# A hybrid decoder step on one core: three stages merged into one program per engine, and the attention's value product with its operands exchanged

## The reference, cut to what matters

```python
h = x @ w_in                                    # 1024 -> 8 x 512
# mixer A: 8 heads of 64; for (window, dilation) in (128,1), (512,4), (2048,16):
s = q @ k.T * ATTN_SCALE + rel_bias             # keys at distances 0, d, 2d, ..., window
p = exp(s - max(s)); out = (p / den) @ v        # the three merged by their denominators
# mixer B: 4 heads, state 128x128, gated linear recurrence
S = diag(f_t) @ S + outer(1 - f_t, i_t);  o_t = S.T @ q_t
y = LayerNorm(ALPHA * x + concat(attn * silu(ga), rms(o_b) * silu(gb)) @ w_out)
```

## Time and profile before

| | |
|---|---|
| time, median of 3 runs | 1592.22 us (1588.28 to 1593.67) |
| the profiled execution's own time | 1593.84 us |
| its span, from the first to the last instruction | 1592.0 us |
| mean granted TensorE clock | 0.969 |
| PE busy | 1531.7 us (96%) |
| DVE busy | 767.2 us (48%) |
| ACT busy | 503.4 us (32%) |
| POOL busy | 440.9 us (28%) |
| stage 2's last product | 854.08 us |
| stage 3's first and last product | 857.27 and 1065.87 us |
| stage 4's first product | 1068.51 us |

### The profile page before, as it was taken

One profiled execution on the slowest core, in us unless ns is written; L12 is line 12 of the kernel. 1 busy time (PEld: TensorE's weight loads), 2 busy tenths in 40 slices (PEclk: granted clock), 3 DMA queues, 4 the chain that ended last, 5 costly groups with the idle time before them and its releaser, 6 DMA issues. The chain is left out here.

```text
span 1592.0 us, 25593 instructions
## 1 busy us (share of the span) xinstructions
PE 1531.7 (96%) x9830; PEld 1374.3 (86%) x9830; DVE 767.2 (48%) x1941; ACT 503.4 (32%) x1426; POOL 440.9 (28%) x281
## 2 busy tenths in 40 slices
PE   7999999998999999899998999989899999899998
PEld 7999999996788777677787999979899999788886
DVE  6022110004323224121214699847677777698885
ACT  5111111113200114122322032337677777423321
POOL 1233210000330000000001000018987779344443
PEclk9999999998999999999999599989999999999999
DMA  9999996233786957866665547859696971866642
GB/s 308 338 329 350 343 318 187 81 117 124 210 291 191 313 200 261 299 213 207 202 205 140 114 157 220 257 185 236 138 207 150 202 183 63 286 207 214 219 158 78
DMA packets 174501, 338.34 MB, mean 213 GB/s; under 512 B 15635, under 2 KB 115283, under 8 KB 165523
## 3 DMA queue, kind: packets, MB, share of 16 engines
q1 hardware_dynamic: 141452, 169.18, 35.0%
q10 hardware_dynamic: 22432, 111.29, 22.0%
q0 software_dynamic: 10512, 56.48, 13.3%
HBM read 262.25 MB, written 155.39 MB: 262 GB/s over the span
## 5 line engine op out<-in xcount | busy, mean ns | idle before, releaser
L1394 POOL CAST a_sorted<-a_plain 128x2048 fp32r<-128x2048 f32 x45 | 171.6, 3872 | 240.5 <-POOLq L932 204.8
L251 PE MATMUL acc<-xhi,whi 128*128 128x424 f32 (+1 forms) x640 | 227.3, 355 | 8.6 <-DVE xlo L230 8.6
L759 PE MATMUL nacc<-nwhi,nxhi 128*128 128x512 f32 (+1 forms) x544 | 219.5, 403 | 13.5 <-DVE nwlo L494 7.3
L251 PE MATMUL acc<-xlo,whi 128*128 128x424 f32 (+1 forms) x640 | 226.9, 355 | 0.0
L251 PE MATMUL acc<-xhi,wlo 128*128 128x424 f32 (+1 forms) x640 | 226.8, 354 | 0.0
L759 PE MATMUL nacc<-nwlo,nxhi 128*128 128x512 f32 (+1 forms) x544 | 214.5, 394 | 0.0
L759 PE MATMUL nacc<-nwhi,nxlo 128*128 128x512 f32 (+1 forms) x544 | 214.5, 394 | 0.0
L1659 ACT ACTIVATE a_prob<-a_prob,a_stage 128x256 f32<-128x256 f32 (+1 forms) x384 | 174.1, 454 | 84.2 <-DVE a_stage L1501 81.9
L1501 DVE CUSTOM_DVE_ANT_0 a_prob<-a_banks,a_bias 128x256 f32<-128x256 f32 (+1 forms) x384 | 125.4, 364 | 82.0 <-PE a_banks L1759 73.5
L1784 PE MATMUL a_banks<-a_v,a_probT 128*128 128x64 f32 x1200 | 157.7, 269 | 4.4 <-DVE a_probT L1513 4.4
L1784 PEld LDWEIGHTS a_banks<-a_v,a_probT 128*128 128x128 f32 x1200 | 150.1, 193 | 5.8 <-DVE a_probT L1513 5.0
(11 more groups left out here) (215 smaller groups left out, 2547.3 us busy)
## 6 DMA issues: line engine op xcount, KB each, us to landing
a_plain<-split_qk POOLq DMA_DIRECT2D x48, 512.0 KB, 12.5
out_kwin_s<-in_cache_kT ACTq DMA_DIRECT2D x8, 2048.0 KB, 19.3
split_qk<-spare POOLq DMA_DIRECT2D x16, 1024.0 KB, 14.6
spare<-in_xT SPq DMA_DIRECT2D x32, 512.0 KB, 7.1
projN<-nstage SPq DMA_DIRECT2D x32, 512.0 KB, 6.6
qg<-in_cache_kT ACTq DMA_DIRECT2D x8, 2048.0 KB, 10.6
kf<-in_cache_v ACTq DMA_DIRECT2D x8, 2048.0 KB
out_kwin_s<-in_cache_kT ACTq DMA_DIRECT2D x8, 2032.0 KB, 28.6
```

The costliest lines, as they stand in the source:

```text
L251: mm = pe.matmul(acc[:, j, 0:n], w[:, u, k], x[:, k, c0:c0 + n], start=(k == 0 and a == 0), stop=(k == KD - 1 and a == 2))
L759: mm = pe.matmul(acc[0:m, n % 2], x[:, u, k, 0:m], w[:, k, g * H:(g + 1) * H], start=(k == 0 and b == 0), stop=(k == KD - 1 and b == 2))
L1394: nc.gpsimd.tensor_copy(dst[:, n].rearrange("p (r m) -> p r m", r=d), src[:, n].bitcast(F32).rearrange("p (m r) -> p r m", r=d)).then_inc( ...
```

## The change

It has two main parts and some that go with them.

- Stages 2, 3 and 4 no longer have a `Block` each. Each function returns its five streams as a `Stage`, and `build` opens one `Block` in which every engine runs the streams of the three stages one behind the other. The tiles in PSUM become one shared tile of eight banks, and waits that the meeting points had made needless are written out.
- In `values` the value tile (128 keys x 64) is stationary and the transposed probabilities (128 keys x 128 queries) move. The first block of a unit writes to partitions 0 to 63 and the second to 64 to 127, which are two column halves of the array, and products of the two halves alternate. Four units fill one bank with results that have the queries on the columns. ACT copies it to `oT` (`keep_turned`), PE transposes it in four pieces (`turn_back`) to the same bank, and then `evacuate` copies it to `stage` as before, one step later than before.
- `warm_up` is gone. The scores of the first three attention units are issued by the recurrence's tail, between its last `read_out`s. There the four `turn_keys` of the last segment have a bank each and are issued in a row, and the `delta`s run two ahead. The squares of the last segment's output (`late_squares`) are done by ACT in attention steps 2 to 5.
- SP issues `load_weights(7)` right behind `load_weights(6)`. POOL begins to sort for head 0 while the last segment of the recurrence runs.
- The last `turn_back` stands inside `project(0)`, and ACT's last `evacuate` behind `recurrent_part(1)`.

```diff
-        with nc.Block() as block:
-            @block.tensor
-            def _(pe):
+        def tensor(pe):
...
+        return Stage(sync, gpsimd, vector, scalar, tensor)
...
+        with nc.Block() as block:
...
+            @block.tensor
+            def _(pe):
+                natural.tensor(pe)
+                recurrence.tensor(pe)
+                attention.tensor(pe)
...
                 def turn_keys(s, c):
                     pe.wait_ge(upd_done, NU * (s + 1))
-                    if i >= 1:
+                if s < NSEG - 1 and i >= 1:
                         pe.wait_ge(khn_done, i)
+                if s == NSEG - 1:
+                    pe.wait_ge(khn_done, NCK * s) if c == 0 else pe.wait_ge(mask_done, NA * NSEG - 3 + c)
                     for h in range(HB):
-                        mm = pe.transpose(t_ps[:, h * P:(h + 1) * P], kd[u][:, h, c * CH:(c + 1) * CH], ident[:])
+                    mm = pe.transpose(turned(s, c)[:, h * P:(h + 1) * P], kd[u][:, h, c * CH:(c + 1) * CH], ident[:])
...
                     turn_keys(NSEG - 1, c)
-                for c in range(NCK):
+            for c in range(2):
                     delta(NSEG - 1, c)
+            for c in range(NCK):
                     read_out(NSEG - 1, c)
+                if c + 2 < NCK:
+                    delta(NSEG - 1, c + 2)
+                if c < NCK - 1:
+                    keep["first_scores"](pe, c)
...
                 load_weights(6)
+            load_weights(7)
                 store_partials(NG - 1, 2)
...
                 load_partials(1)
-                load_weights(7)
                 load_gates(2)
...
+            def keep_turned(m):
+                act.wait_ge(pv_done, 4 * (m + 1))
+                if m >= 1:
+                    act.wait_ge(back_done, m)
+                nc.scalar.activation(oT[:].rearrange("p j d -> p (j d)"), o_ps[:, m % 2], ACT.Copy).then_inc(ot_done, 1)
+
                 def evacuate(n):
                     h, c, b = units[n]
-                    act.wait_ge(pv_done, n + 4)
+                act.wait_ge(back_done, n // 4 + 1)
...
-                    if n >= 8 and n % 4 == 0:
-                        evacuate(n - 8)
+                if 2 <= n < 2 + NCK:
+                    first["late_squares"](n - 2)
+                if n == NU + 3:
+                    round_mix(0)
+                if n >= 7 and n % 4 == 3:
+                    keep_turned(n // 4 - 1)
+                if n >= 9 and n % 4 == 1:
+                    evacuate(n - 9)
...
-                    for a, (w, vt, _) in enumerate(ts):
-                        col = (2 * (n % 4) + w) * DA
-                        mm = pe.matmul(o_ps[:, (n // 4) % 2, col:col + DA], probT[:, n % 3, a],
-                                       v[g % 2][:, c, vt, x * DA:(x + 1) * DA],
-                                       start=(a == 0 or ts[a - 1][0] != w), stop=(a == len(ts) - 1 or ts[a + 1][0] != w))
+                first_of = [next(a for a, t in enumerate(ts) if t[0] == w) for w in range(2)]
+                for a, (w, vt, _) in sorted(enumerate(ts), key=lambda t: (t[0] - first_of[t[1][0]], t[1][0])):
+                    mm = pe.matmul(o_ps[w * DA:(w + 1) * DA, (n // 4) % 2, n % 4 * P:(n % 4 + 1) * P],
+                                   v[g % 2][:, c, vt, x * DA:(x + 1) * DA], probT[:, n % 3, a],
+                                   start=(a == first_of[w]), stop=(a == len(ts) - 1 or ts[a + 1][0] != w))
                     mm.then_inc(pv_done, 1)
+            def turn_back(m):
+                pe.wait_ge(ot_done, m + 1)
+                for j in range(4):
+                    mm = pe.transpose(o_ps[:, m % 2, j * P:(j + 1) * P], oT[:, j], ident[:])
+                mm.then_inc(back_done, 1)
...
                 pe.wait_ge(const, 16)
-                warm_up()
-                for n in range(NU + 4):
-                    if n < NU:
-                        scores(n)
+            for n in range(2, NU + 4):
+                if 3 <= n < NU:
+                    scores(pe, n)
...
+                if n >= 9 and n % 4 == 1:
+                    turn_back(n // 4 - 2)
```

More of the change, by code:

```diff
@@ L6 @@
+from collections import namedtuple
 from contextlib import ExitStack
@@ L1173, in attend_and_project @@
+        return Stage(sync, gpsimd, vector, scalar, tensor)
+def attend_and_project(nc, split_qk, projN, rep_p, w_o, attn_s, o_b, norm_g, partials, x_all, ln_g, ln_b, y, copied, first, keep):
     NBK = T // P
@@ L1219, in attend_and_project @@
         probT = sb("a_probT", [P, 3, 4, P])
+        oT = keep["oT"]
         bias.append(sb("a_bias1", [P, 2, NC, 2 * P]))
@@ new lines, in scores @@
+        def scores(pe, n):
+            h, c, b = units[n]
+            g, x = divmod(h, 2)
+            if c == 0 and b == 0:
+                pe.wait_ge(pair_landed[x], 96 * (g + 1))
+            if c > 0 and b == 0:
+                pe.wait_ge(sort_done, 6 * h + 3 * c)
+            source = plain[x] if c == 0 else sorted_[c - 1] if h < HALVES - 1 else (plain[0], sorted_[0])[c - 1]
+            if n < 3:
+                pe.wait_ge(keep["mask_done"], 18 * NSEG)
+                pe.wait_ge(keep["khn_done"], NCK * NSEG)
+            else:
+                pe.wait_ge(p_done, n - 2)
+            for w in range(2):
+                q0, k0, m = block_keys(c, b + w)
+                for a in range(2):
+                    mm = pe.matmul(s_ps[:, n % 3, w * 2 * P + (2 - m) * P:(w + 1) * 2 * P],
+                                   source[:, 0, q0:q0 + P], source[:, 1 + a, k0:k0 + m * P],
+                                   start=(a == 0), stop=(a == 1))
+            mm.then_inc(s_done, 1)
@@ L1849, in _ @@
-                for _ in range(FILL):
-                    pe.matmul(z_ps[1][:, 0, 0:P], ident[:], ident[:], start=True, stop=True)
-                for p in range(1, LAST):
-                    project(p)
-                project_last()
+                            mm = pe.matmul(z_ps[w][:, g], m[:, w, k], ww[:, g * H:(g + 1) * H],
+                                           start=(k == 0 and a == 0), stop=(k == KD - 1 and a == 2))
+                    mm.then_inc(last_half if g == 0 else z_done, 1)
@@ new lines, in tensor @@
+            pe.wait_ge(const, 16)
+            for n in range(2, NU + 4):
+                if 3 <= n < NU:
+                    scores(pe, n)
+                if n == NU + 1:
+                    transposes(0)
+                if 2 <= n < NU + 2:
+                    turn(n - 2)
+                if n >= 4:
+                    values(n - 4)
+                if n >= 9 and n % 4 == 1:
+                    turn_back(n // 4 - 2)
+            project(0)
+            transposes(1)
+            pe.wait_ge(o_out, NU // 4)
@@ L1856, in build @@
+            for _ in range(FILL):
+                pe.matmul(z_ps[1][:, 0, 0:P], ident[:], ident[:], start=True, stop=True)
+            for p in range(1, LAST):
+                project(p)
+            project_last()
+        return Stage(sync, gpsimd, vector, scalar, tensor)
 def build(nc, a, o):
@@ L1876, in build @@
             keep[n] = [sem(f"k_{n}{u}") for u in range(m)]
+        for n in ("q1_done", "a_done", "mask_done", "khn_done", "hs_done", "ho_done"):
+            keep[n] = sem(f"h_{n}")
+        for n in ("group_done", "w_split", "x_split"):
+            first[n] = sem(f"n_{n}")
+        first["sem"] = sem
         right = region(whole, nc)[0]
@@ L1879, in build @@
             keep[n] = right(f"k_{n}", [P, T // P, HB], side="right")
+        first["bounds"], first["ident"] = right("bounds", [P, 4, HB], side="right"), right("ident3", [P, P], side="right")
+        NLM = len(PLEVELS)
+        masks = right("masks", [P, NLM + 2, CH // 2], I32, side="right")
+        first["lmask"], first["dmask"] = masks[:, 0:NLM], masks[:, NLM:NLM + 2].rearrange("p a t -> p (a t)")
+        keep["oT"] = masks[:, 0:8].rearrange("p a t -> p (a t)").bitcast(F32).rearrange("p (j d) -> p j d", j=4)
         with ExitStack() as ctx:
```

2437 lines of the change are left out of this document (1217 added, 1220 removed).

## The result

The changed kernel takes 1607.42 us (median of 4 runs, 1605.88 to 1609.64), the kernel before, with its runs beside it, 1590.25 us. The ratio is 1.0104 with a 95% interval from 1.0090 to 1.0119: slower by 17.2 us. The forecast was 1601 us in a range from 1568 to 1622, and slower with a chance of .60. The profiled execution took 1605.88 us with a span of 1604.1 us. Stage 2, with the same products on PE, shows where such a difference comes from: it takes between 465.3 and 470.5 us in the thirteen traces of this case.

The account below looks back on a forecast made before the run. PE was taken to bound the attention, busy 284.32 of 290.00 us. Terms 25.6 - 2.5 - 3.7 + .5 - 6.8 - 4.0 = +9.1 on 1593.84 gave 1602.9, or 1601 us against the median; range 1568 to 1622.

Parts of the forecast that it names:

- Exchanged value product, +25.6: Attention on PE: four-tile units unchanged, three-tile units +.24 and two-tile units +.25 us, with a .34 us switch per unit.
- Two passes of two halves in one slot: Value products on PE: two passes in different column halves take .11 us together, so a four-tile unit needs 4 slots, .44.
- The rival without overlap: Value products on PE: the halves do not overlap and every pass costs .11 us, 61.6 us more, 1663 us; chance .08.
- The stall at heads 1 to 2, -2.5: VectorE's 4.70 us wait for a partial result's store shrinks as two-tile units get longer; -2.5 us, between 0 and -8.
- First seam, -3.7: PE between stages 2 and 3: 2.96 of the 3.19 us gap go, and about .7 more at the first scores.
- The +.5 for the exit work: The earlier stage's exit work moves to the seam in front of stage 2, costing .5 us.
- Second seam, -6.8: Recurrence to attention: first attention transposes 7.7 us sooner, of which late squares on ACT may take .9 back; -3 to -9.
- End, -4.0: End of attention: PE's 4.17 us wait goes with the eighth weight piece issued earlier, less .45 for `turn_back`; 0 to -5.
- Partly hidden switch: Rival: the weight load into the idle half proceeds while the other drains, .16 us less a unit, 1570 us; chance .17.
- The swap with column tiles as the simply right form for 64 columns: Rival: value passes halve without any switch cost, -38 in place of +25.6 us, 1538 us; chance .05.
- The low clock of the first segment: Rival: PE's .50 clock in the recurrence's first segment ends, 8.4 us less, 1592 us, no change; chance .12.
- The merging brings nothing: Rival: the seams' waits turn into waits for data, 11.5 us more than forecast, 1613 us; chance .08.

Follow-up runs that it names:

- The pairs: Changed kernel with the value products of two units issued together every second step, so the array is divided 96 times instead of 192: 1595.74 us, ratio 1.0027.
- The one-line experiment: Changed kernel with the load of the eighth output weight piece put back behind the loads of row block 1: one run, 1613.20 us.
- the merging alone: Changed kernel with the value product as before (probabilities stationary, no copy or turn back), all the merging kept: 1592.17 us, ratio 1.0008.
- the late version: Changed kernel with POOL's first sort put back behind the recurrence's last store: 1601.33 us, ratio 1.0064.

## Why the prediction was right, and where its sum was not

The direction was right, the time within the range and 6.4 us above the forecast. The mechanism that the forecast named, switches of the divided array, is the one that makes the change slow. But that the sum came near was luck: two errors opposed each other, an attention 8 us too dear and 17 us of losses that had no term. Point by point:

- **Exchanged value product, +25.6.** Mis-sized. An ordinary head (2 to 5) grew by 2.3 to 2.5 us where the terms give 5 x .24 + 8 x .25 = 3.2. In the rows shown, four-tile units became .02 shorter (forecast 0) and two-tile units .22 longer (.25; .20 by the median of all their plain steps). The plain steps of three-tile units, over twenty in each trace, have a median of 1.47 us before and 1.58 after, 1.68 with the turn back's share: .21 longer (.24). Without the waits for stores all heads together are +19.6. The switch price of .34 is right for four tiles, .09 + .15 + .10, of which before had .08 in its own exposed load; in two-tile units, where the scores have 128 columns, the last term is .05. The pairs give .32 by a second way. What I took from products of the sampled step with 512-column neighbours held to .02 between 128-column ones. Three-tile units were not read from a row but put midway between the others; that was near enough (1.45 for 1.47). The .8 us a head sit in no one kind of unit.
- **Two passes of two halves in one slot.** Right, 4 slots are .44. That they had to alternate, as the change does it, turned out not to matter. The rival without overlap fell.
- **The stall at heads 1 to 2, -2.5.** Mis-sized: head 1 is 4.3 us shorter than before where its neighbours are 2.4 longer, 6.7 us in all, since longer two-tile units hide the store and the low clock behind it does not come. In the changed kernel 1.5 us of the wait of 4.70 in the earlier trace rows were left.
- **The attention in all**: forecast 23.1, measured 19.6 - 6.7 + 1.7 (first units) = 14.7.
- **First seam, -3.7.** Right: 2.95 at the seam itself, and the first 32 score passes behind it take 3.46 us in all eleven merged traces where the two unmerged ones have 4.26 and 5.16 (.7 forecast). The +.5 for the exit work is not resolved: stage 2 begins at 383.4 to 385.7 us in the thirteen traces, merged or not.
- **Second seam, -6.8.** -3.12 and -4.88, 8.0 us; the late squares took their time in the first units and not here. That the attention's early scores brought ACT's table load to the front of the chain was as worked out.
- **End, -4.0.** -3.4: the wait went (-4.8), 1.3 us came at the first output product. The one-line experiment shows that the move of `load_weights(7)` did it.
- **The step that failed** is the change's part on POOL. The prediction prices what ACT gets and SP's moved load and has no term for `sort(0, 1)`, whose new place stood in the change's description: it was put at nothing without a reason. In the last segment VectorE was already busy 3.96 of 4 us (the window of before at 1019), and 12.4 us of casts were put beside it. The Trainium skill has the rule, in "SBUF — State Buffer", section "SBUF: two separate sides": VectorE and GpSimd share a pair of ports as an exclusive lock that is held for a whole instruction, and a VectorE operation with two SBUF inputs takes part in it against a GpSimd operation that reads SBUF. The traces agree: .68 us stretched to 4.36 and 4.17 us, the second and third cast took 4.34 and 4.25 us where the first took 3.89, and in the recurrence's tail, where VectorE's state updates read one operand from PSUM, the same casts cost nothing. The sort's place cost 12.15 us in the trace, 10.6 in the medians.
- **POOL's drain, +4.5,** was not foreseen and could not be read as a cost from the page of before, where the drain at the end of stage 4 is hidden behind the last store and that of stage 2 under PE. In a trace it shows as the length of a waiting engine's last record.
- **The rivals.** Partly hidden switch: fell, .32 is paid. The swap with column tiles as the simply right form for 64 columns, the rule of the Trainium skill's page "TensorEngine Tiling (Array Packing)", section "Performance Considerations": the passes halve as it implies, but a division between every two full-width stages costs more than they give; with half the divisions the attention is 20 us shorter. (The prediction's 59 us for this rival do not follow from the two values that it names: 88 x .37 + 64 x .14 + 40 x .15 is 48 us, and 63 with the .08 of exposed load that each old unit pays; less the turn back's 21 that is near its other bound, -40.) The low clock of the first segment stayed at .50. "The merging brings nothing" came out nearest by its number, 1613, and by its result: 1.0008 alone. But not by its reason. In the trace of the merging alone the seams and the end gave 2.95 + 3.13 + 4.88 + 5.75 = 16.7 us, and 12.2 + 4.5 = 16.7 were lost at two other places of it. With these repaired the merging alone is worth 15 us.

The median's 17.2 us against the trace's 12.1: of the -3.97 in the table, 3.0 lie in stage 2 ahead of the first sampled step, where the changed kernel's trace has 67.0 us, the late version's 66.8, and the eleven others, before among them, 69.9 to 71.1. The other 1.0 lies behind it, where before has 400.5 and the others 397.7 to 399.5. So most of it is no effect of the change; the unmerged kernel with the new value product has -2.1 there too.

## What to carry to other kernels

When stages are merged, list for each engine what may now run beside what: work that was free behind a meeting point (a sort, a drain) may land on the chain of another engine, or behind the last store. Splitting TensorE's array between full-width products is paid by the switch and not by the product: count switches, and put as many divided products behind each other as the buffers allow. And a sum that comes near the measured time proves nothing term by term: here 8 us too much and 17 us not foreseen stood on both sides of it.

## What the runs showed of the hardware

- Passes in two column halves run side by side whatever their order: all of one half and then all of the other took .59 us, alternating .59, and six passes, two against four, also .59.
- Casts on POOL from SBUF to SBUF stretched VectorE's products of two SBUF operands from .68 us to 4.36 and 4.17, and left state updates with one PSUM operand at 1.12 us for four.
- POOL's drain took 4.5 us for stage 4 alone, 9.6 for stages 2 to 4, and 5.0 where one of 4.6 stood between, with POOL's last transfer issued 177 us before the inserted one and over 300 us before those at the end.
- A hold-up of 8.7 us on VectorE cost 12.15 us, and one of 4.38 us cost 10.9: PE had stood still, and its granted clock was .50 to .58 for the 10 us that followed.
